# Two token tiles of an output projection moved between the last attention steps, and its second-half weights split earlier

## What is computed

```python
def one_block(inp):
    qn, qr, blk = inp
    s = (jnp.einsum('bqhd,bkhd->bhqk', qn, k_nope)
         + jnp.einsum('bqhd,bkd->bhqk', qr, k_rope)).astype(jnp.float32) * scale
    q_chunk = (blk * Q_BLOCK + jnp.arange(Q_BLOCK)) // CHUNK
    s = jnp.where(key_chunk[None, :] <= q_chunk[:, None], s, -jnp.inf)
    p = jax.nn.softmax(s, axis=-1).astype(v.dtype)
    return jnp.einsum('bhqk,bkhv->bqhv', p, v)
...
return chunk_causal_attention(q_nope, q_rope, k_nope, k_rope, v) @ w_out
```

## Time and profile before

| | us |
|---|---|
| runs, median (lowest to highest) | 1253.67 (1250.55 to 1256.56) |
| profiled execution, its own time | 1254.26 |
| its span | 1252.5 |
| TensorE busy | 1206.7 (96% of the span) |
| VectorE busy | 663.4 (53%) |
| ScalarE busy | 532.0 (42%) |
| mean granted TensorE clock | 0.99 of full |

### The profile page before, as it was taken

The page is one execution under the profiler, slowest core; times in us unless marked ns, Lnnn a source line. Parts: engine busy times, 40 slices in busy tenths (PEclk is TensorE's granted clock), DMA queues, the critical chain, the costliest instruction groups (busy, mean ns, idle before and its releaser), DMA issues.

```text
span 1252.5 us, 16277 instructions
## 1 busy us (share of the span) xinstructions
PE 1206.7 (96%) x5995; PEld 995.9 (80%) x5995; DVE 663.4 (53%) x1028; ACT 532.0 (42%) x1049; POOL 114.3 (9%) x129
## 2 busy tenths in 40 slices
PE   6899999999999999999999998989999999999997
PEld 5677788887988888888888777767988888888886
DVE  4576867875663443443447257753653443443444
ACT  4554555454542332323436765543542332332332
POOL 2231212310380000000000000100000000000000
PEclk9999899999999999999999999999999999999999
DMA  4332121133333323323232122202323323333221
GB/s 122 102 84 56 47 67 52 51 119 126 101 101 102 94 96 96 100 100 87 98 101 77 54 79 61 68 18 68 101 101 101 99 92 96 100 100 89 95 85 68
DMA packets 87492, 108.23 MB, mean 86 GB/s; under 512 B 9186, under 2 KB 48195, under 8 KB 87428
## 3 DMA queue, kind: packets, MB, share of 16 engines
q1 hardware_dynamic: 85684, 101.85, 26.2%
q0 software_dynamic: 1744, 5.51, 1.4%
HBM read 104.20 MB, written 2.10 MB: 85 GB/s over the span
## 4 chain that ended last, share of the span: by engine, by line
PE 83%; DVE 7%; ACT 6%; issue 2%; DMA 1%; POOL 0%; DVEq 0%; SPq 0%; ACTq 0%
PE bank L1479 25%; PE bank L1481 25%; PE bank L1480 24%; PE pp L1621 1%; PE po L1899 1%; PE pp L1522 1%; PE pp L1479 1%; PE pp L1480 1%; PE pp L1481 1%; ACT w_hi L491 1%; ACT w_hi L489 1%; PE pp L1880 1%; DVE xl L1136 0%; DVE stat L1442 0%; PE po L1632 0%
## 5 line engine op out<-in xcount | busy, mean ns | idle before, releaser
L1479 PE MATMUL bank<-h_lo,w_hi 128*128 128x512 f32 (+4 forms) x572 | 218.5, 382 | 9.0 <-DVE h_lo L1079 4.4
L1480 PE MATMUL bank<-h_hi,w_lo 128*128 128x512 f32 (+4 forms) x572 | 215.3, 376 | 0.0
L1481 PE MATMUL bank<-h_hi,w_hi 128*128 128x512 f32 (+4 forms) x572 | 215.0, 376 | 0.0
L1479 PEld LDWEIGHTS bank<-h_lo,w_hi 128*128 128x128 f32 (+1 forms) x572 | 106.8, 187 | 31.4 <-issue 5.4
L1479 PE MATMUL bank<-wx,a_hi 128*128 128x512 f32 x320 | 126.3, 395 | 2.6 <-DVE wx L499 2.6
L1308 DVE TENSOR_TENSOR tmp<-sq,bank 128x512 f32<-128x512 f32 x64 | 44.0, 687 | 156.3 <-ACT sq L910 156.3
L1480 PE MATMUL bank<-wx,a_lo 128*128 128x512 f32 x320 | 125.2, 391 | 0.0
L910 ACT ACTIVATE sq<-bank 128x512 f32<-128x512 f32 x64 | 38.3, 598 | 204.6 <-PE bank L1481 204.6
L1481 PE MATMUL bank<-wx,a_hi 128*128 128x512 f32 x320 | 125.2, 391 | 0.0
L1481 PEld LDWEIGHTS bank<-h_hi,w_hi 128*128 128x128 f32 (+1 forms) x572 | 106.7, 187 | 19.9
L1479 PE MATMUL bank<-w_lo,a_hi 128*128 128x512 f32 x304 | 119.6, 394 | 2.5 <-DVE a_lo L1198 1.6
(11 more groups left out here) (312 smaller groups left out, 2059.3 us busy)
## 6 DMA issues: line engine op xcount, KB each, us to landing
stage<-in_mlp_w SPq DMA_DIRECT2D x128, 512.0 KB, 3.6
stage<-in_ev_w_in SPq DMA_DIRECT2D x28, 512.0 KB, 3.8
stage<-in_ev_w_out SPq DMA_DIRECT2D x8, 512.0 KB, 3.6
stage<-in_od_w_out SPq DMA_DIRECT2D x8, 512.0 KB, 3.5
stage<-in_od_w_in SPq DMA_DIRECT2D x10, 256.0 KB, 3.0
x_tok<-in_x SPq DMA_DIRECT2D x4, 512.0 KB, 4.8
xr<-in_x POOLq DMA_DIRECT2D x4, 512.0 KB, 3.8
gbc<-in_norm_gains POOLq DMA_DIRECT2D x4, 512.0 KB, 4.3
```

The source lines that it names most:

```text
L1479: nc.tensor.matmul(dst, wh, xl_, start=first, stop=False)
L1480: nc.tensor.matmul(dst, wl, xh, start=False, stop=False)
L1481: return nc.tensor.matmul(dst, wh, xh, start=False, stop=last)
```

## The change

It does three things. Of the 28 head products of `oo_first` (heads 0 to 6 of four tiles), 12 are moved into steps 24 to 33 of the attention loop, between the scores and the transposes of a step; a table says which. Behind the loop heads 6 of t = 0 and 1 come, then `values(7)`, then t = 2 and 3. And the splits of units OO + 5 to OO + 7, which ScalarE and VectorE made one behind each of the tiles q = 0, 1, 2, now stand with that of OO + 4 directly behind the last `att_out`.

```diff
                     token_square(j, t, h, src, eps[:, 0:1])
-                    if q < 3:
-                        if j == 2:
-                            split_high(act, u0 + q + AHEAD)
-                    elif q < 2 * NT - 1:
+                    if 3 <= q < 2 * NT - 1:
                         split_high(act, next_u + q - 3)
...
             att_out(MLA_HEADS - 1)
-            split_high(act, OO + SPLIT)
+            for u in range(SPLIT):
+                split_high(act, OO + SPLIT + u)
             linear_out("oo", 2, OO, MLP[1][1])
...
+            OO_FILL = {24: [(0, 0), (1, 0)], 25: [(0, 1)], 27: [(1, 1), (0, 2)], 28: [(1, 2)], 29: [(0, 3), (1, 3)],
+                       31: [(0, 4), (1, 4)], 32: [(0, 5)], 33: [(1, 5)]}
             for j in range(4 * MLA_HEADS + 2):
                 if j < 4 * MLA_HEADS:
                     scores(j)
...
+                for t, o in OO_FILL.get(j, ()):
+                    out_head("oo", 2, t, o, OO_ORDER)
                 if 2 <= j:
                     transposes(j - 2)
...
             def oo_first():
-                for o in range(KD - 1):
-                    out_head("oo", 2, 0, o, OO_ORDER)
+                for t in range(2):
+                    out_head("oo", 2, t, KD - 2, OO_ORDER)
                 values(MLA_HEADS - 1)
-                for t in (1, 2, 3):
+                for t in (2, 3):
                     for o in range(KD - 1):
                         out_head("oo", 2, t, o, OO_ORDER)
```

More of the change, by code:

```diff
@@ L1470, in _ @@
             att_out(MLA_HEADS - 1)
-            split_low(dve, OO + SPLIT)
+            for u in range(SPLIT):
+                split_low(dve, OO + SPLIT + u)
             linear_out("oo", 2, OO, MLP[1][1])
```

## The result

The changed kernel takes 1239.32 us in the median (1238.19 to 1241.51) against 1252.56 (1250.55 to 1256.56) before: ratio 0.9898, 95% interval 0.9879 to 0.9916. It is faster, by 13.2 us of the medians, where 10.3 were forecast (1243.5 us, range 1240.5 to 1249.5): the time lies 1.2 us under the range. Two later comparisons of the same two kernels gave 0.9907 (0.9871 to 0.9942) and 0.9907 (0.9889 to 0.9926), 11.5 and 11.3 us between the medians.

The account below looks back on a forecast made before the run. TensorE, busy 96% of the span, was taken to bound the kernel, with waits in two places. Gains of 5.4 + 4.9 = 10.3 us gave 1244.0 from 1254.26, 1243.4 from the median; forecast 1243.5 us, range 1240.5 to 1249.5.

Parts of the forecast that it names:

- Term A: Attention's last steps: moved head products fill TensorE's pauses, gaining 5.4 us, bounds 3 and 6.5.
- the wait at step 24: TensorE waits 0.8 us before the head product of t = 1, whose bank VectorE still reads for head 7's query.
- that at the values: At the values after step 25's scores, about 0.6 us of waiting for ScalarE's copy of the transposes stays.
- entries: First matmuls behind one of another kind take longer: eight at 0.08 us cost 0.6 us in the attention's last steps.
- The seven pauses: TensorE's pauses from 818 to 840 us: 5.8 us, with 0.2 more each covered by modelled ends, 7.2 us.
- My overlay: New order laid step by step over old times in the attention's last steps: 6.3 us gained; the lower 5.4 was kept.
- Term B: Second half of the output projection: earlier splits remove the weights' wait and low clock, gaining 4.9 us, bounds 2.5 and 4.9.
- the range's best case: Both places gain their upper bounds, 6.5 + 4.9 = 11.4 us; with the runs' spread it sets the range's low end, 1240.5.
- 1 (only the second place pays): Fill pushes the softmax chain back and pauses return in the attention's last steps: gain there about 0.5, 1248.3 us, chance 0.12.
- 2 (the bank): At the second half's start the wait moves from weights to the bank: gain there 2.5, time 1245.8 us, chance 0.15.
- 3 (a fall of the clock makes it slower): New short waits lower the clock through the projection: 1289 us if all its matmuls are slow, chance 0.03.
- 4 (given back in the MLP): MLP loads come late and TensorE waits there, losing most of the gain: about 1250 us, chance 0.05.

Follow-up runs that it names:

- the table without waits: Changed kernel with the twelve products spread otherwise (step 24 one, 25 three, 26 one, 27 none): 1238.09 us, ratio 0.9889; in five later rounds 1237.94 us, 0.9901.
- the products alone: Kernel before with only the twelve head products moved, the splits of `linear_out` as before: 1244.9 us, ratio 0.9936.
- the splits alone: Kernel before with only the splits moved directly behind the last `att_out`, the products as before: 1247.2 us, ratio 0.9964.
- two early: Kernel before with only OO + 4 and OO + 5 split behind the last `att_out`, OO + 6 and OO + 7 behind squares q = 0 and 1: 1251.32 us.
- three products: Changed kernel with only the three products of steps 24 and 25 moved, the other nine behind the loop: 1249.88 us.

## Why the prediction was wrong, step by step

What bounds: right. TensorE waited in two places, and nothing was given back behind them.

Term A, step by step: the wait at step 24 was 0.57 us in the profile's bracket (about 0.7 from start to start; forecast 0.8) and that at the values 0.30 (about 0.5; forecast 0.6). Nine products met no wait, as laid out. The first matmul of a product took 0.29 us behind scores (817.16 to 817.45), 0.06 over its price, where 0.08 was forecast. What was mis-sized is what there was to fill. The forecast net of entries was 7.2 + 0.2 - 0.6 = 6.8 us; the table without waits shows 7.3. The seven pauses do cost 7.2 us when their starts are measured against the same places after the change. But I left out shorter waits that have no bracket, two above all: the transposes at 832.76 start 0.36 us behind the mask, those at 823.97 0.21, where 0.06 is usual after the change, so 0.30 and 0.15 us. With 1.2 instead of 1.4 us left, A came out 6.1 instead of 5.4. My overlay had said 6.3, and I kept the lower number; the overlay was the better reading.

Term B: right, 5.06 for 4.9, and 0.1 over what I had called the most, since the undisturbed second half takes 24.47 us and not 24.6. But its size hangs on the clock: the same pause cost 29.53 - 24.47 = 5.1 us where the clock fell behind it, in all three profiles of the kernel before, and 28.35 - 24.47 = 3.9 where it did not (the products alone).

The sum of the two stretches is 11.2, inside the range's best case of 11.4. The forecast time was missed by 4.2 us: 0.9 are the two terms, 1.1 the base (a median of three, 1253.67, that stood at 1252.56 in the comparison itself), 0.1 rounding, and 2.1 are in neither stretch. So what failed is the step from the sum to the time. It took one base and one difference of stretches as if they stood still, and put everything outside the two stretches at nothing. The range's low end was 1253.7 - 11.4 = 1242.3 with 1.8 us for the spread of the runs; the measured 1239.32 lies 3.0 under 1242.3.

The further comparisons show in its place mostly scatter. The median of before was 1252.56, 1251.92 and 1250.89 in the three (the later two on different chips), that of the changed kernel 1239.32, 1240.46 and 1239.58. The differences are 13.2, 11.5 and 11.3 us: over the 11.2 of the stretches they stand by 2.1, 0.3 and 0.1. Each interval is wider than that; the last, 0.9889 to 0.9926, is 9.3 to 13.9 us.

Whether a part of the excess, 0.8 us in the mean of the three, is real stays open. A candidate is the clock in the first stretch. It fell in four of the six profiles of kernels that keep pauses there (the third of before, the splits alone, two early, three products), at 0.6 to 1.6 us each, and in none of the seven that have all twelve products. Each fall begins in the four transposes behind a pause: once behind that of 1.57 us, three times behind those of 1.33 and 0.55 us. Averaged over the six that is 0.9 us, over the three profiles of the kernel before alone 0.5. This was seen and counted, not tested by an experiment of its own.

The rivals: 1 (only the second place pays) fell with 6.11 us in the first. 2 (the bank) was not met. 3 (a fall of the clock makes it slower) had the sign wrong as far as 13 profiles tell: the falls stand behind pauses, and the change takes pauses away. 4 (given back in the MLP) was not met: 358.67 and 358.74 us. The rule of program order in the Trainium skill ("TensorE: Matmul & The Clock Gate", Part 2) held in the trace: VectorE had divided the probabilities of step 22 by 817.98, and their transposes, behind the waiting product, started at 819.44.

## What to carry to other kernels

Where an engine waits in many short pauses, lay the new order over the old times step by step and do not set it aside for the sum of the recorded pauses: that sum leaves out the waits that have no bracket, and was the worse of the two here (6.3 and 5.4 forecast, 6.1 measured). For weights that must be split before use, ask when their staging buffer is emptied: here one load was late because the split that empties its buffer stood behind a square that had nothing to do with it, and with two splits moved the next load was late for the same reason. And a forecast to 0.1% needs the scatter of its base and of the difference: several profiles and comparisons of the same kernels, not one.

## What the runs showed of the hardware that was not expected

Equal code ahead of the change took between 812.13 and 819.58 us from the start to step 24 over the profiles, 7.4 us apart. Windows of two profiles, before and after the change, at the same place:

```profile
140.00:145.00 5.00, 3.09 (x26) 2.78 (x28) 5.00 (x8) 2.57 (x6) 1.10 (x1) 0.70 0.00 0
145.00:150.00 5.00, 5.00 (x33) 4.10 (x32) 4.97 (x12) 0.62 (x1) 0.42 (x1) 0.62 0.39 110
```

```profile
140.00:145.00 5.00, 4.75 (x52) 3.89 (x52) 4.96 (x10) 2.48 (x7) 0.00 (x0) 1.00 0.15 37
145.00:150.00 5.00, 5.00 (x23) 3.71 (x21) 5.00 (x12) 1.51 (x4) 2.42 (x3) 1.00 0.25 72
```

In the first a wait of 1.91 us (TensorE for VectorE's `rinv`, until 142.69) and a granted clock of 0.62 to 0.70 stand where the second has a wait of 0.17 us and a clock of 1.00. The clock also fell in the attention's last steps, where no pause has a bracket over 1.6 us, in some executions and not in others of the same instructions: a pause's price has a part that changed from run to run.
